# GpSimd's constant transfers start after the first weights, and the turned memory leaves PSUM ahead of the sine

## What is computed

```python
h = rms_norm(x, g_mix)                       # x: 256 x 1024
proj = h @ w_in                              # split into c_kv, k_rope, q_gla, k_gla, a_gla, q_mla, ...
c_kv, k_rope, q_gla, k_gla, a_gla, q_mla, ... = split(proj)
k_pe = apply_rope(rms_norm(k_rope, g_k_rope), cos, sin)      # cos, sin of positions * inv
kv = rms_norm(c_kv, g_ckv) @ w_ukv
...                                          # causal attention over 8 heads: masked scores, softmax
log_a = log_sigmoid(a_gla @ w_gla_gate + b_gla_gate) / 16    # gated linear attention, in levels
kv_m = rms_norm(mem, g_mem) @ w_mem_kv       # mem: 256 x 1024, attention over a memory
...
x = x + (gates * branches) @ w_o
x = x + square(relu(rms_norm(x, g_ffn) @ w_up)) @ w_down
```

## Time and profile before

| what | value |
|---|---|
| median of three runs | 1018.98 us (1018.76 to 1019.25) |
| the profiled execution | 1019.29 us |
| its span, first to last instruction | 1017.1 us |
| TensorE busy | 997.9 us, 98% of the span |
| VectorE, ScalarE, GpSimd busy | 515.5, 203.0, 26.1 us |
| moved by DMA | 139.66 MB |
| granted TensorE clock over the span | 1.000 |

### The profile page before, as it was taken

One profiled execution on the slowest core, in us unless ns is written; L12 is line 12 of the kernel. 1 busy time (PEld: TensorE's weight loads), 2 busy tenths in 40 slices (PEclk: granted clock), 3 DMA queues, 4 the chain that ended last, 5 costly groups with the idle time before them and its releaser, 6 DMA issues.

```text
span 1017.1 us, 11262 instructions
## 1 busy us (share of the span) xinstructions
PE 997.9 (98%) x4596; PEld 598.2 (59%) x4596; DVE 515.5 (51%) x1090; ACT 203.0 (20%) x407; POOL 26.1 (3%) x39
## 2 busy tenths in 40 slices
PE   5999999999999999999999999999999999999998
PEld 3854444664555448988844459448844444568443
DVE  1602731227567831799755561788966751432211
ACT  3303322222323112212000011101012221453000
POOL 3000000000000005000000000000000000000000
PEclk9999999999999999999999999999999999999999
DMA  9441642244235237444244534424243344211721
GB/s 286 168 166 41 219 153 82 83 166 148 101 94 166 90 111 225 166 166 166 84 166 170 185 131 167 174 83 166 83 166 106 143 166 156 92 42 43 248 83 41
DMA packets 66706, 139.66 MB, mean 137 GB/s; under 512 B 2864, under 2 KB 6208, under 8 KB 66656
## 3 DMA queue, kind: packets, MB, share of 16 engines
q1 hardware_dynamic: 64736, 134.56, 38.3%
q0 software_dynamic: 1712, 4.32, 1.9%
q10 hardware_dynamic: 208, 0.08, 0.0%
HBM read 137.90 MB, written 1.05 MB: 137 GB/s over the span
## 4 chain that ended last, share of the span: by engine, by line
PE 93%; DMA 3%; ACT 1%; DVE 1%; SPq 0%; issue 0%; DVEq 0%; ACTq 0%
PE pair L1441 72%; PE pair L1687 5%; PE turned L1382 3%; PE score L1687 3%; DMA arena<-in_mem 2%; PE turned L1687 1%; PE score L1834 1%; DMA ring<-in_w_in 1%; PE score L1778 1%; PE score L1847 1%; PE score L1546 1%; PE score L1595 1%; PE score L1545 1%; PE score L1611 1%; PE turned L1765 0%; PE turned L1767 0%
## 5 line engine op out<-in xcount | busy, mean ns | idle before, releaser
L1441 PE MATMUL pair<-ring,hT 128*128 128x512 f32 (+2 forms) x1024 | 442.9, 587 | 3.6 <-DMA ring<-in_w_in 3.6
L1441 PEld LDWEIGHTS pair<-ring,hT 128*128 128x128 f32 x1024 | 191.7, 191 | 217.7 <-issue 212.6
L740 DVE TENSOR_TENSOR arena<-arena 128x512 f32<-128x512 f32 (+9 forms) x339 | 215.4, 652 | 93.1 <-ACT arena L449 38.0
L1441 PE MATMUL pair<-hT,ring 128*128 128x256 f32 (+2 forms) x1232 | 217.1, 337 | 0.2 <-ACT hT L488 0.2
L1441 PEld LDWEIGHTS pair<-hT,ring 128*128 128x128 f32 (+1 forms) x1232 | 191.7, 190 | 22.8 <-issue 2.1
L1441 PE MATMUL pair<-ring,arena 128*128 128x512 f32 (+1 forms) x224 | 90.6, 562 | 0.0
L449 ACT ACTIVATE arena<-pair 128x512 f32<-128x512 f32 (+2 forms) x70 | 38.9, 581 | 214.3 <-PE pair L1441 214.3
L878 DVE CUSTOM_DVE_ANT_0 arena<-score,masks 128x256 f32<-128x256 f32 (+2 forms) x40 | 18.1, 451 | 124.1 <-PE score L1546 65.9
L1441 PEld LDWEIGHTS pair<-ring,arena 128*128 128x128 f32 x224 | 42.1, 190 | 44.3 <-issue 43.5
L459 ACT ACTIVATE arena<-turned 128x512 f32<-128x512 f32 (+2 forms) x66 | 32.7, 536 | 139.8 <-PE turned L1382 139.8
L1382 PEld LDWEIGHTS turned<-ident,arena 128*128 128x128 f32 (+1 forms) x363 | 42.6, 144 | 25.0 <-issue 15.8
(11 more groups left out here) (192 smaller groups left out, 602.0 us busy)
## 6 DMA issues: line engine op xcount, KB each, us to landing
ring<-in_w_in SPq DMA_DIRECT2D x33, 2048.0 KB, 8.6
ring<-in_w_up SPq DMA_DIRECT2D x8, 2048.0 KB, 9.0
ring<-in_w_down SPq DMA_DIRECT2D x8, 2048.0 KB, 8.0
ring<-in_w_o SPq DMA_DIRECT2D x4, 2048.0 KB, 8.1
ring<-in_w_mem_kv SPq DMA_DIRECT2D x2, 2048.0 KB, 8.4
ring<-in_w_glu SPq DMA_DIRECT2D x2, 2048.0 KB, 8.3
ring<-in_w_ssm_out SPq DMA_DIRECT2D x2, 2048.0 KB, 7.9
ring<-in_w_ukv SPq DMA_DIRECT2D x4, 512.0 KB, 3.8
```

Of the source, the lines that this page charges most:

```text
L740: return dve.tensor_tensor(o, a, b, op)
L1441: ins = pe.matmul(o_, s, m, start=a, stop=b)
```

## The change

GpSimd now waits until the first weights (`weights0`) have landed before it starts any transfer. The frequencies, positions, the gate's weight and the gains come first in its order; the masks and the levels follow them and signal a semaphore of their own, `masks_in`. VectorE waits for `masks_in` ahead of the first masked scores. The two waits for `consts_in` count two transfers less. On ScalarE the output of `ckv` and the turned memory are taken out of PSUM before the wait for `angle` and the sines.

```diff
@@ -387,8 +387,7 @@  (GpSimd)
-            pool.dma_start(masks[:, :, :], d["c_masks"]).then_inc(sem("consts_in"), 16)
-            pool.dma_start(levels.rearrange("p (l n) -> p l n", n=32), d["c_levels"]).then_inc(sem("consts_in"), 16)
+            pool.wait_ge(sem("weights0"), 16)
             pool.dma_start(inv[:, :], d["c_inv"]).then_inc(sem("consts_in"), 16)
@@ -398,6 +397,8 @@
                 pool.dma_start(gain[name], src.to_broadcast([P, w])).then_inc(sem("consts_in"), 16)
+            pool.dma_start(masks[:, :, :], d["c_masks"]).then_inc(sem("masks_in"), 16)
+            pool.dma_start(levels.rearrange("p (l n) -> p l n", n=32), d["c_levels"]).then_inc(sem("masks_in"), 16)
@@ -505,13 +506,13 @@  (ScalarE)
+            ck = ckv.rearrange("p (t c) -> p t c", c=RANK + ROPE)
+            take("ckv", lambda t: ck[:, t, :], cols=RANK + ROPE)
+            for t in range(TT):
+                turned_rows(t, memT3, "g_mem")
             act.wait_ge(sem("angle"), 1)
             link(act.activation(rope[:, 1, :, :], rope[:, 1, :, :], ACT.Sin))
             act.activation(rope[:, 0, :, :], rope[:, 0, :, :], ACT.Sin).then_inc(sem("rope_ready"), 1)
-            ck = ckv.rearrange("p (t c) -> p t c", c=RANK + ROPE)
-            take("ckv", lambda t: ck[:, t, :], cols=RANK + ROPE)
-            for t in range(TT):
-                turned_rows(t, memT3, "g_mem")
@@ -784,7 +785,7 @@  (VectorE)
-            dve.wait_ge(sem("consts_in"), 16 * (8 + len(GAINS)))
+            dve.wait_ge(sem("consts_in"), 16 * (6 + len(GAINS)))
@@ -900,6 +901,7 @@  (VectorE)
+            dve.wait_ge(sem("masks_in"), 32)
@@ -1497,7 +1499,7 @@  (TensorE)
-            pe.wait_ge(sem("consts_in"), 16 * (8 + len(GAINS)))
+            pe.wait_ge(sem("consts_in"), 16 * (6 + len(GAINS)))
```

More of the change, by code:

```diff
@@ L143 @@
     "x_in0": "first tile of x", "x_in1": "second tile of x", "mem_in": "the memory", "ident_in": "the identity",
-    "rows_in": "parameters that become columns", "consts_in": "masks, gains, positions and the gate's weight",
+    "rows_in": "parameters that become columns", "consts_in": "gains, positions and the gate's weight", "masks_in": "masks and levels",
     "bgate0": "bias of the even gates", "bgate1": "bias of the odd gates", "ssm_in": "state space parameters",
@@ L506, in _ @@
                 row_norm(t, mem_tok[:, DM * t:DM * t + DM], 4, "mem", junk)
-            act.wait_ge(sem("angle"), 1)
-            link(act.activation(rope[:, 1, :, :], rope[:, 1, :, :], ACT.Sin))
-            act.activation(rope[:, 0, :, :], rope[:, 0, :, :], ACT.Sin).then_inc(sem("rope_ready"), 1)
             ck = ckv.rearrange("p (t c) -> p t c", c=RANK + ROPE)
@@ L514, in _ @@
                 turned_rows(t, memT3, "g_mem")
+            act.wait_ge(sem("angle"), 1)
+            link(act.activation(rope[:, 1, :, :], rope[:, 1, :, :], ACT.Sin))
+            act.activation(rope[:, 0, :, :], rope[:, 0, :, :], ACT.Sin).then_inc(sem("rope_ready"), 1)
             take("gq", lambda t: qgT[:, 512 * t:512 * t + 512], scale=GK ** -0.5)
```

## The result

The changed kernel takes 1013.3 us (median of 4 runs, 1012.8 to 1015.4) where the kernel before takes 1019.1 us beside it; the ratio is 0.9945, with a 95% interval of 0.993 to 0.9959. That is 5.8 us won. The forecast was 4.2 us won, 1014.8 us, with a range of 1013.2 to 1016.9 us: the sign and the places were right, the size was over a quarter too small, and the median stands 0.1 us inside the fast end of the range.

The account below looks back on a forecast made before the run. TensorE, busy 98% of the span, was taken as the bound, so only its early waits could go: 2.69 + 0.3 + 1.2 = 4.2 us won, from the median 1019.0 to 1014.8 us, range 1013.2 to 1016.9 us.

Parts of the forecast that it names:

- Where the time could be had: TensorE's waits ahead of 44.77 us; everything behind shifts by what is won before it.
- (1): Start of the first product, ckv: GpSimd's wait removes the 2.69 us pause, x gains 0.3 us; start at 13.6 us.
- the late bound: Latest estimated landing of ckv's first weights, 13.1 us; the early bound was 9.3 us.
- (4): Transposes of the memory's second tile before gk: ScalarE's new order empties their banks sooner, 1.2 us won.
- (3): SP's DMA queues: gq's weights taken to land at 22 us, the memory at 27 us, by sharing with GpSimd's transfers.
- Rival (B): The memory, landing at 28.7 us, binds gk's start: 3.1 us won, 1015.9 us; chance 0.20.
- (A): TensorE's clock in the first product: late rise, 2.7 us won, chance 0.10; early rise, 5 to 6 us, chance 0.12.
- the trace speaks for neither: Within the clock rival: the only evidence, 5.4 us of slow matmuls after an idle stretch, favours neither late nor early rise.
- (C): First weights come no earlier, their own short rows being slow: only 1.2 us won, 1017.8 us; chance 0.08.
- (D): GpSimd's packets delay gq and the memory; slower, 1022.2 us if memory lands at 35 us; chance 0.05 including cases towards (C).

Follow-up runs that it names:

- e5: The changed kernel without GpSimd's wait for the first weights, masks and levels still last: 1016.6 us, ratio 0.9968 to the kernel before.
- e1: The changed kernel with ScalarE's old order, sines ahead of the turned memory (GpSimd's part alone): 1014.2 us, ratio 0.9944 to the kernel before.
- e2: The kernel before with only ScalarE's new order, GpSimd's transfers as before: 1017.2 us, ratio 0.9972 to the kernel before.
- e6: The changed kernel with masks and levels issued first behind GpSimd's wait: 1013.9 us, ratio 0.9944 to the kernel before.
- e3: The changed kernel with TensorE held before the first product by an extra, unused ScalarE pass: 1016.8 us, ratio 0.9974 to the kernel before.
- e7: The changed kernel with unread identity products keeping TensorE busy while it waits for x: 1011.3 us, ratio 0.9919 to the kernel before.
- e4: The kernel before with six extra identity products in the pause ahead of the first product: 1020.6 us, ratio 1.0007 to the kernel before.
- e9: The kernel before with six extra identity products in the first pause and ScalarE's new order: 1017.2 us, ratio 0.9971 to the kernel before.
- e8: e7 with eight more such products, ahead of the identity's landing, on a block of ones: 1011.6 us, ratio 0.992 to the kernel before.
- e10: e7 with ScalarE's old order, sines ahead of the turned memory: 1012.7 us, ratio 0.9927 to the kernel before.
- e11: The changed kernel run once more, unaltered: 1014.1 us, ratio 0.9942 to the kernel before.

## Why the prediction was right, and where it was short

- *Where the time could be had* was right: two pauses of TensorE ahead of 45 us, and a shift of everything behind them. The span confirms it to 0.1 us.
- *(1), the first product's start*, 2.69 + 0.3 us predicted, 2.99 us measured. The weights landed at 12.3 us, nearer to the late bound of 13.1 than to the 10 us taken; that was close to 13.6 us, and e5 shows that with the wait left out it would not have been enough. That the 0.3 us came out is luck. Only 0.1 of it is `x`'s: ScalarE's first square and the second tile's transposes came 0.1 us earlier. The rest is that the first matmul starts at 13.57 us, ahead of the modelled end of the last transpose at 13.78 us.
- *(4), the second transposes*, 1.2 us predicted, 1.19 measured. The size was right and its cause only half: e1 shows that with GpSimd's part in place the pause goes without ScalarE's reordering. The prediction treated the two parts as independent terms, though its own chain (memory, square, norm, angle, sine) ran through the transfer that part (1) moved. On the kernel before the order is worth its 1.2 us at that place (e2); on the change, nothing that can be measured. This hangs on the next term: before, the second bank was free 15.3 us behind the memory's landing (44.11 - 28.77), which with the memory at the predicted 27 us makes 42.3 us, while the prediction had TensorE asking for the banks at 39.7 us (an estimate: `gk` at 40.6 less 0.87). With that landing the reordering would have been needed.
- *(3), the queues*, was the term that was mis-sized: the memory at 27 us taken and 24.5 to 28.7 us as bounds, 21.3 us measured. Two steps failed. GpSimd's transfers were counted as taking their share from 10 us on, but they were issued from 12.6 us, and even the positions, 0.5 KB each, took 5.1 us from issue to landing; and the 1.15 MB of masks, levels and biases, issued from 19.6 us on, came behind the memory all but altogether: 0.13 MB of GpSimd's 1.66 had moved when it landed. (The count of bytes left out `gk`'s weights too: SP's queue had moved 6.86 MB before and 6.57 MB after by then, where `x`, the first weights, `gq`'s and the memory are 5.5 MB.) e6 puts the masks back in front of the rest, and the memory slips by 3.4 us. Rival (B), the memory as the bound, is refuted with a reserve of 4.6 us in the change (30.16 - 4.2 - 21.35) and 0.8 us in e6. The Trainium skill, DMA: Bandwidth & Descriptors, section on queues, rings and completion order, says that each DMA engine takes turns between its queues, packet by packet. The prediction read from it that the crowding moves onto `gq` and the memory; the trace shows them landing 8.1 and 7.4 us earlier, ahead of the crowd. In the crowd of 9.5 to 12.5 us before, SP's and GpSimd's queues had 54% and 53% of the engines' time, which is even, but with 399 and 127 packets; no run here shows in what order the packets went.
- *(A), the clock.* The sum let the slow stretch of 5.4 us move along unchanged. It shrank to about 2.2 us, which is the missing 1.62 us, and the early rise had been given 0.12. The step that failed is "the trace speaks for neither": a single trace in which the slow stretch follows a pause can't tell a fixed cost from one that belongs to the pause. e3 and e7 show that it belongs to what TensorE did before. So 4.2 us of the 5.8 are the forecast's own, and 1.6 us are this rival's, which had a chance of 0.12.
- *(C)* fell with the landing at 12.3 us. *(D)* had the memory slip; it came 7.4 us earlier. The landing of the memory (25 to 28.7 us) and `gk` at 40.6 us, named as signs, both came out earlier, at 21.3 and 38.8 us. The earlier memory only made a reserve larger; it was the clock that took the result to within 0.1 us of the edge of the range.

## What to carry to other kernels

A wait removed from a cold TensorE is worth more than its length: the matmuls behind it run faster too, here by 1.6 us for 2.7 us of pause (1.1 for 2.4 in e3), as long as nothing else binds behind them (e4), and a handful of products that nobody reads, in a time in which TensorE waits anyway, brings the rest (2.0 us here). Transfers that nobody needs for 30 us should be issued behind those that bound the start; here it took a wait, the order of the list was not enough (e5). And where two edits touch one chain, cost the second on the profile that the first would leave: reordering ScalarE won 1.2 us at its place alone and nothing after the other edit.

## What the runs showed of the hardware

- The product's slow stretch shows in the spacing of matmuls only; the granted clock read 1.00 while they ran at half pace (11.3 against 8.6 us for the same 32 matmuls).
- Issue on SP is held up by a crowd as well: the instruction that issues the memory's load took 5.04 us before and 2.00 us after.
- GpSimd's small and spread transfers cost the DMA engines far more time than their bytes: 53% of it for 0.15 of 0.66 MB in 9.5 to 12.5 us before, at 219 GB/s in all; 408 GB/s at the same share without them.
- The landing of the first weights differs from trace to trace with the same transfers: 15.3 to 16.4 us with GpSimd's list as before (before, e2, e4, e9), 11.4 to 12.7 us behind GpSimd's wait (the change, e1, e3, e6, e7, e8, e10, e11).
